# Splitting the squares of every query and key tile of the two dilated mixers into two fp32r parts, with the sum and the norm one share later

## The chip, the cores and the metric

One core of a Trainium2 chip runs the whole program. The metric is the device time of one execution in microseconds, the median of three runs. TensorE (PE) multiplies matrices, VectorE (DVE), ScalarE (ACT) and GpSimd (POOL) do the elementwise work, and SyncE (SP) issues the weight loads. Each engine works through its own instructions in order and waits on semaphores.

## The reference

The model is a trunk of four layers on 512 tokens of width 1024. The token mixers of layers 0 to 3 are dilated window attention (A), sparse attention (B), gated DeltaNet (C) and A again; each layer ends in a squared-ReLU MLP. The change concerns only the queries and keys of the A mixers, which are normalised per head:

```
def rms_norm(x, gain):
    y = x * lax.rsqrt(jnp.mean(x * x, axis=-1, keepdims=True) + EPS)
    return y * gain

def mixer_a(h, w_in, q_gain, k_gain, w_out, bias_tab):
    qkv = (h @ w_in).reshape(B, S, 3, A_N_GROUPS, A_HEADS, HEAD_DIM)
    q = rms_norm(qkv[:, :, 0], q_gain)
    k = rms_norm(qkv[:, :, 1], k_gain)
    v = qkv[:, :, 2]
    for g, (window, dilation) in enumerate(A_GROUPS):
        o, lse = dilated_window_attention(q[:, :, g], k[:, :, g], v[:, :, g], ...)
    wts = softmax(lses over the three groups)
    return sum(wts * outs) @ w_out
```

## The kernel before

**Weights.** A chunk of fp32 weights is loaded into `raw`. ACT copies it to `w_hi` in fp32r (L777, `rounding`), and POOL puts the rest, `raw - w_hi`, into `w_lo` in four pieces (L620, `split`). A product is then three fp32r matmuls for each block: `w_hi` with the high part of the activations, `w_hi` with the low part, and `w_lo` with the high part (L1916 in the A mixer).

**An A mixer.** There are four pairs of heads. Each pair has six tiles of 128 x 512: a query and a key tile for each of three groups, so 24 tiles in a mixer. The first six ("opening") and the values come first. The other 18 tiles are then projected between the steps of the attention. I number them tile 0 to tile 17, in order. A tile is 24 matmuls. The work is cut into 52 *shares* G of 8 or 9 matmuls, two in each *step* s of the attention loop: `fill(2s)` and `fill(2s+1)`. A tile ends in every third share, with two exceptions: the 18 tiles end in shares 2, 5, 8, 11, 14, 17, 20, 23, 25, 28, 31, 34, 37, 40, 43, 46, 49 and 51. `a_ended(i, G)` names the tile that ends in share G.

**A step on PE** is: `weigh(s-3)` (probabilities times values, L2205), `scores(s)` (L2162 near, L2169 far), `turn(s-2)` (transposes, L2189), `fill(2s)`, `fill(2s+1)`, then in some steps from 26 on a piece of the output projection (`joined`, L1962), and in steps 9, 17, 25 and 33 `difference` (L2219), which spreads the log-sum-exps of a pair's groups over `stat_bank`, PSUM bank 7. Step 28 has no filling work, and in steps 27 and 29 it is only `joined`.

**The norm of a tile**: ACT squares it from PSUM into the one buffer `asq`, that is `sq0` (L902, `qk_tile`), and copies the tile itself out (L903). DVE adds the epsilon term in place (L1378, `add_eps`). PE sums the squares over each head with a matrix of 128 x 128 (`sum_qk`). ACT takes the logarithm and then the exponential with -0.5 (L927 and L929, `qk_rms`), and POOL multiplies the tile by the result (L634, `qk_scale`). In the 18 tiles of the steps the sum is one fp32 matmul (L2092), issued at the end of the share after the one in which the tile ends. In the six opening tiles ACT makes an fp32r copy of the squares (L920, `sq_high`) in a spare slice of `g_hi`, DVE writes the rest (L1384, `sq_low`) to `g_lo`, and PE sums the two with two fp32r matmuls (L2088, L2089).

**`stat_bank` is shared.** A sum waits until the logarithm of the tile before has read the bank (`qln_done`), and after a `difference` until DVE has read it (`aclamp_done`, L1433, `clamped`). A `difference` waits for the logarithm of the last sum issued.

**The order around the steps on ACT**: copies of turned probabilities (L1017, from step 26), `probs(s)` (the exponentials of the attention, L977), in steps 10, 18, 26 and 34 three operations of 128 x 512 that make the mixing weights of a pair (L1026, L1028, L1030), `part(2s)`, `part(2s+1)`, and in steps 12, 20, 28 and 36 the high part of the pair's output (L1035). `part(G)` does the norm of the tile that ended a share before, then squares and copies the tile that ends in G, then rounds the next weights if a chunk is done. On DVE a step is: reciprocals (L1410), from step 25 on the scaling of probabilities (L1441), outputs (L1420), `logits(s)` (L1401), `part(2s)`, copies of turned probabilities up to step 25 (L1501), `part(2s+1)`, `clamped`, low part of the output (L1460).

## Time and profile before

| | |
|---|---|
| median of 3 runs | 2767.97 us (2767.09 to 2771.35) |
| the profiled execution | 2773.47 us, of which the span from first to last instruction is 2771.7 us |
| PE busy | 2716.1 us, 98% of the span |
| POOL / ACT / DVE busy | 1359.7 (49%) / 1086.8 (39%) / 1046.8 us (38%) |
| chain that ended last | PE 91%, DVE 3%, ACT 2%, POOL 2% |
| fp32 sums L2092 | 72 matmul records for the 36 sums of the two A mixers, 592 ns each |

Two matmul records make up one fp32 sum. A record's length contains the way through the array, so neighbouring records overlap; what a matmul costs PE is read from the distance of the starts or from the chain. Times of the trace count from the start of the span. In layer 0 the steps run from 130.7 us to about 330 us.

### The profile page before, as it was taken

What the parts mean: (1) busy time and instruction counts of PE and PEld (TensorE: products, weight loads), DVE (VectorE), ACT (ScalarE), POOL (GpSimd) and SP (SyncE); (2) the same over time, 40 slices, a digit from 0 to 9 for tenths busy, and PEclk for the clock granted to TensorE, in tenths of its full rate; (3) what the DMA queues carried; (4) which work ended last, traced back from release to release, by engine and by line L of the source; (5) the groups of instructions that cost most, each with busy time, mean ns of one, the idle gap of its engine ahead of it and who ended that gap; (6) DMA issues with size and microseconds to landing.
All of it is one profiled execution on the core that took longest, in us unless ns stands there. A gap on an engine that the chain in (4) does not pass through costs nothing.

```text
span 2771.7 us, 37296 instructions
## 1 busy us (share of the span) xinstructions
PE 2716.1 (98%) x14594; PEld 2193.4 (79%) x14594; DVE 1046.8 (38%) x1966; ACT 1086.8 (39%) x1649; POOL 1359.7 (49%) x1042
## 2 busy tenths in 40 slices
PE   8999999999999999999899999999999999999999
PEld 6977688888766788888788887888888977688887
DVE  4044622113486512213777874311123044622112
ACT  5355633223446423324334344322234355533222
POOL 4577354445455354445444442445455576345443
PEclk9999999999999999999899999999999999999999
DMA  4322122323422123223312110232323322122232
GB/s 143 99 69 63 52 92 91 106 91 92 106 46 77 61 92 106 91 91 110 80 33 57 37 62 24 92 98 91 106 91 99 100 54 69 56 97 91 92 105 76
DMA packets 273439, 227.87 MB, mean 82 GB/s; under 512 B 29220, under 2 KB 260388, under 8 KB 273300
## 3 DMA queue, kind: packets, MB, share of 16 engines
q1 hardware_dynamic: 262578, 216.66, 25.9%
q10 hardware_dynamic: 10722, 9.28, 1.5%
q8 instruction: 96, 1.57, 0.2%
q14 instruction: 43, 0.35, 0.0%
HBM read 223.62 MB, written 2.30 MB: 82 GB/s over the span
## 4 chain that ended last, share of the span: by engine, by line
PE 91%; DVE 3%; ACT 2%; POOL 2%; issue 1%; DMA 1%; ACTq 0%; SPq 0%; DVEq 0%; POOLq 0%
PE bank L2009 50%; PE bank L1916 20%; PE bank L2132 4%; PE bank L2372 2%; PE bank L2512 2%; PE bank L2092 1%; PE bank L2189 1%; PE bank L2205 1%; POOL w_lo L620 1%; PE bank L1962 1%; PE bank L2169 1%; PE bank L2162 1%; PE bank L2219 1%; POOL arena L693 1%; PE bank L1943 1%
## 5 line engine op out<-in xcount | busy, mean ns | idle before, releaser
L620 POOL TENSOR_TENSOR w_lo<-raw,w_hi 128x512 fp32r<-128x512 f32 x808 | 1081.0, 1368 | 1087.0 <-ACT w_hi L777 1067.7
L777 ACT ACTIVATE w_hi<-raw 128x2048 fp32r<-128x2048 f32 x201 | 383.7, 1909 | 462.1 <-PE bank L2009 423.3
L2009 PE MATMUL bank<-h_hi,w_hi 128*128 128x512 f32 x1024 | 400.8, 391 | 0.0
L2009 PE MATMUL bank<-g_hi,w_hi 128*128 128x512 f32 x1024 | 398.6, 389 | 0.0
L2009 PE MATMUL bank<-h_hi,w_lo 128*128 128x512 f32 x1024 | 398.4, 389 | 0.0
L2009 PE MATMUL bank<-g_hi,w_lo 128*128 128x512 f32 x1024 | 398.4, 389 | 0.0
L2009 PE MATMUL bank<-h_lo,w_hi 128*128 128x512 f32 x1024 | 398.4, 389 | 0.0
L2009 PE MATMUL bank<-g_lo,w_hi 128*128 128x512 f32 x1024 | 398.4, 389 | 0.0
L1916 PE MATMUL bank<-h_hi,w_hi 128*128 128x512 f32 x776 | 317.3, 409 | 2.4 <-POOL w_lo L620 1.9
L1916 PE MATMUL bank<-h_lo,w_hi 128*128 128x512 f32 x776 | 310.5, 400 | 0.0
L1916 PE MATMUL bank<-h_hi,w_lo 128*128 128x512 f32 x776 | 307.8, 397 | 0.0
L847 ACT ACTIVATE arena<-arena 128x512 f32<-128x512 f32 x128 | 80.9, 632 | 425.8 <-DVE arena L1345 425.8
L1345 DVE SCALAR_TENSOR_TENSOR arena<-bank,rs 128x512 f32<-128x512 f32 x128 | 88.5, 691 | 372.7 <-PE bank L2009 349.2
L1360 DVE TENSOR_TENSOR x<-x,bank 128x512 f32<-128x512 f32 x96 | 66.0, 687 | 431.6 <-PE bank L2009 431.6
L2009 PEld LDWEIGHTS bank<-h_hi,w_hi 128*128 128x128 f32 x1024 | 192.2, 188 | 41.0 <-issue 1.4
L2009 PEld LDWEIGHTS bank<-h_lo,w_hi 128*128 128x128 f32 x1024 | 192.2, 188 | 41.0 <-issue 1.4
L2009 PEld LDWEIGHTS bank<-h_hi,w_lo 128*128 128x128 f32 x1024 | 192.2, 188 | 40.2
L2009 PEld LDWEIGHTS bank<-g_hi,w_lo 128*128 128x128 f32 x1024 | 192.2, 188 | 40.2
L2009 PEld LDWEIGHTS bank<-g_lo,w_hi 128*128 128x128 f32 x1024 | 192.2, 188 | 39.8
L2009 PEld LDWEIGHTS bank<-g_hi,w_hi 128*128 128x128 f32 x1024 | 192.2, 188 | 39.7
L1916 PEld LDWEIGHTS bank<-h_hi,w_hi 128*128 128x128 f32 x776 | 147.5, 190 | 40.0 <-issue 10.4
L1916 PEld LDWEIGHTS bank<-h_lo,w_hi 128*128 128x128 f32 x776 | 147.6, 190 | 35.1 <-issue 6.9
(276 smaller groups left out, 3805.0 us busy)
## 6 DMA issues: line engine op xcount, KB each, us to landing
raw<-in_mlp_w SPq DMA_DIRECT2D x128, 1024.0 KB, 5.4
raw<-in_a_w_in SPq DMA_DIRECT2D x48, 512.0 KB, 5.1
raw<-in_c_w_in SPq DMA_DIRECT2D x32, 512.0 KB, 5.5
raw<-in_a_w_in SPq DMA_DIRECT2D x12, 1024.0 KB, 5.2
raw<-in_b_w_in SPq DMA_DIRECT2D x18, 256.0 KB, 4.0
raw<-in_a_w_out SPq DMA_DIRECT2D x4, 1024.0 KB, 4.9
raw<-in_b_w_in SPq DMA_DIRECT2D x4, 1024.0 KB, 5.4
arena<-bias_scratch ACTq DMA_DIRECT2D x16, 256.0 KB, 3.6
```

Source lines behind the costliest of these rows:

```text
L620: ins = nc.gpsimd.tensor_tensor(w_lo[s][:, k, :], raw[s][:, k, :], w_hi[s][:, k, :].bitcast(F32), ALU.subtract)
L693: nc.gpsimd.tensor_tensor(btm[t % 2][:, :, 0:n], bbias[f % 2][:, :, TOK - n:TOK], score[b].unsqueeze(1).to_broadcast([P, 2, n]), ALU.add). ...
L777: nc.scalar.activation(w_hi[s][:], raw[s][:], ACT.Copy).then_inc(w_hi_done, 1)
L847: nc.scalar.activation(gsq[j % 2], relu_t[j % 2], ACT.Square).then_inc(gsq_done, 1)
L1345: nc.vector.scalar_tensor_tensor(relu_t[j % 2], lin_bank[j % 2][:], 0.0, rs, ALU.max, ALU.mult).then_inc(relu_done, 1)
L1360: nc.vector.tensor_tensor(x[:, c, :], x[:, c, :], lin_bank[c % 2][:], ALU.add).then_inc(x_added, 1)
L1916: mm = nc.tensor.matmul(o, lhsT, rhs, start=start, stop=stop)
L1943: mm = nc.tensor.matmul(stat_bank[:], ones, sq[c % 2], start=c == 0, stop=c == CT - 1)
L2009: mm = nc.tensor.matmul(lin_bank[j][:], w[s][:, c, P * j:P * j + P], a[:, c, :], start=c + z == 0, stop=c == CT - 1 and z == 2)
L2132: mm = nc.tensor.matmul(bank[2 + b][:], keys, quads[w][:, c, :], start=half + c + z == 0, stop=half == 1 and c == 3 and z == 2)
L2372: mm = nc.tensor.matmul(out[z:z + HD], lhsT[:, z:z + HD], rhs, start=start, stop=stop)
L2512: mm = nc.tensor.matmul(bk4(3)[:, c, :], atl[k % 3][:, c, :], Tm[:, c, :], start=True, stop=True)
```

## The change

All 24 tiles of an A mixer, and not only the six opening ones, are now summed as two fp32r parts. In the steps the parts are made so: ACT's `sq_high` one share after the tile's end (head of `part`), DVE's `sq_low` behind the copy of turned probabilities of the step (for the tiles of shares 2s-1 and 2s). PE's sum, ACT's `qk_rms` and POOL's `qk_scale` move from one share behind to two. The squaring of the next tile waits for `sq_low` instead of the sum.

```diff
--- before.py
+++ after.py
@@ -240,13 +240,13 @@
             y_first[i] = at_y
             at_y += {0: A_PAIRS, 1: B_PAIRS, 2: C_HEADS}[KINDS[i]]
 
-        opening = {}
+        in_parts = {}
         q_first, copy_first, at_q, at_c = {}, {}, 0, 0
         for i in layers:
             q_first[i], copy_first[i] = at_q, at_c
             if KINDS[i] == 0:
-                for k in range(6):
-                    opening[at_q + k] = len(opening)
+                for k in range(6 * A_PAIRS):
+                    in_parts[at_q + k] = len(in_parts)
             at_q += {0: 6 * A_PAIRS, 1: 10, 2: 0}[KINDS[i]]
             at_c += {0: 12, 1: 8, 2: 2 + 4 * C_HEADS}[KINDS[i]]
 
@@ -449,7 +449,7 @@
 
         def sq_parts(Q):
 
-            return g_hi[:, 4 + opening[Q] % 2, :], g_lo[:, 4 + opening[Q] % 2, :]
+            return g_hi[:, 4 + in_parts[Q] % 2, :], g_lo[:, 4 + in_parts[Q] % 2, :]
 
         def a_stat(f, k):
 
@@ -648,7 +648,7 @@
                                                 ALU.mult).then_inc(an_done, 1)
 
                 def part(G):
-                    for k, n, t in a_ended(i, G - 1):
+                    for k, n, t in a_ended(i, G - 2):
                         qk_scale(0, a_q(i, k, n, t), a_qk_tile(k, t - tile0[n]))
 
                 def share(s, lo, hi):
@@ -894,9 +894,9 @@
                     src, blocks = reversed_blocks(src), by_block
                 act.wait_ge(lin_done, t + 1)
                 sqs = mem[kind]["sq"]
-                if Q in opening:
-                    if opening[Q]:
-                        act.wait_ge(qlo_done, opening[Q])
+                if Q in in_parts:
+                    if in_parts[Q]:
+                        act.wait_ge(qlo_done, in_parts[Q])
                 elif Q - q_base(kind) >= len(sqs) or (Q and len(sqs) == 1):
                     act.wait_ge(ssq_done, Q - len(sqs) + 1)
                 nc.scalar.activation(blocks(sqs[Q % len(sqs)]), src, ACT.Square).then_inc(qsq_raw, 1)
@@ -915,8 +915,8 @@
             def sq_high(Q):
 
                 act.wait_ge(qsq_done, Q + 1)
-                if opening[Q] >= 2:
-                    act.wait_ge(ssq_done, Q - 1 if opening[Q] % 6 >= 2 else Q)
+                if in_parts[Q] >= 2:
+                    act.wait_ge(ssq_done, Q - 1 if in_parts[Q] % (6 * A_PAIRS) >= 2 else Q)
                 nc.scalar.activation(sq_parts(Q)[0], mem[0]["sq"][0], ACT.Copy).then_inc(qhi_done, 1)
 
             def qk_rms(kind, Q):
@@ -963,9 +963,12 @@
 
                 def part(G):
                     for k, n, t in a_ended(i, G - 1):
+                        sq_high(a_q(i, k, n, t))
+                    for k, n, t in a_ended(i, G):
+                        qk(k, n, t)
+                    for k, n, t in a_ended(i, G - 2):
                         qk_rms(0, a_q(i, k, n, t))
                     for x in a_ended(i, G):
-                        qk(*x)
                         ended(*x)
 
                 def probs(u):
@@ -1380,7 +1383,7 @@
             def sq_low(Q):
 
                 hi, lo = sq_parts(Q)
-                dve.wait_ge(qhi_done, opening[Q] + 1)
+                dve.wait_ge(qhi_done, in_parts[Q] + 1)
                 nc.vector.tensor_tensor(lo, mem[0]["sq"][0], hi.bitcast(F32), ALU.subtract).then_inc(qlo_done, 1)
 
             def mixer_a(li, i):
@@ -1499,6 +1502,9 @@
                             dve.wait_ge(apv_done, U0 + u - 2)
                         n = 2 * P * a_blocks(u)
                         nc.vector.tensor_copy(apt[u % 3][:, 0:n], bank[4 + u % 2][:, 0:n]).then_inc(at_copied, 1)
+                    for G in (2 * s - 1, 2 * s):
+                        for k, n, t in a_ended(i, G):
+                            sq_low(a_q(i, k, n, t))
                     part(2 * s + 1)
                     if s == A_UNITS + 3:
                         projected(s - 1)
@@ -2077,13 +2083,13 @@
 
             def sum_qk(kind, Q):
 
-                pe.wait_ge(qlo_done, opening[Q] + 1) if Q in opening else pe.wait_ge(qsq_done, Q + 1)
+                pe.wait_ge(qlo_done, in_parts[Q] + 1) if Q in in_parts else pe.wait_ge(qsq_done, Q + 1)
                 if Q:
                     pe.wait_ge(qln_done, Q)
                 if spread[0]:
                     pe.wait_ge(aclamp_done, spread[0])
                 summed[0] = Q + 1
-                if Q in opening:
+                if Q in in_parts:
                     hi, lo = sq_parts(Q)
                     nc.tensor.matmul(stat_bank[:], halves_r[:], hi, start=True, stop=False)
                     nc.tensor.matmul(stat_bank[:], halves_r[:], lo, start=False, stop=True).then_inc(ssq_done, 1)
@@ -2141,7 +2147,7 @@
                         a, b = max(lo, 24 * j), min(hi, 24 * j + 24)
                         if a < b:
                             tile(n, t, a - 24 * j, b - 24 * j)
-                    for k, n, t in a_ended(i, G - 1):
+                    for k, n, t in a_ended(i, G - 2):
                         sum_qk(0, a_q(i, k, n, t))
 
                 def scores(u):
```

On PE, at the end of step 9 in layer 0 (shares 18 and 19, then the first `difference`), the kernel before has:

```order
L2092 MATMUL bank<-sq,com 128x512 [waits qln_done,qsq_done]
L1916 MATMUL bank<-h_lo,w_hi 128x512
L1916 MATMUL bank<-h_hi,w_lo 128x512
L1916 MATMUL bank<-h_hi,w_hi 128x512
L1916 MATMUL bank<-h_lo,w_hi 128x512
L1916 MATMUL bank<-h_hi,w_lo 128x512
L1916 MATMUL bank<-h_hi,w_hi 128x512
L1916 MATMUL bank<-h_lo,w_hi 128x512
L1916 MATMUL bank<-h_hi,w_lo 128x512
L1916 MATMUL bank<-h_hi,w_hi 128x512
L2219 MATMUL bank<-com,arena 64x128 [waits qln_done,alse_done]
L2219 MATMUL bank<-com,arena 64x128 x15
```

Nine projection matmuls (share 19) stand between the sum of tile 5 and the `difference`. The same place in the changed kernel:

```order
L1922 MATMUL bank<-h_lo,w_hi 128x512
L1922 MATMUL bank<-h_hi,w_lo 128x512
L1922 MATMUL bank<-h_hi,w_hi 128x512
L2094 MATMUL bank<-g_hi,halves_r 128x512 [waits qln_done,qlo_done]
L2095 MATMUL bank<-g_lo,halves_r 128x512
L2225 MATMUL bank<-com,arena 64x128 [waits qln_done,alse_done]
L2225 MATMUL bank<-com,arena 64x128 x15
```

The sum now stands directly ahead of the `difference`. The same has happened in step 25 with the sum of tile 16; at the second `difference`, in step 17, it is the other way round: there the sum of tile 11 stood directly ahead of it, and has moved behind it.

On ACT, steps 25 and 26 of layer 0, that is from the exponentials of step 25 to the norm of tile 17, the kernel before has:

```order
L977 ACTIVATE arena<-arena 128x256 [waits al_done] x2
L927 ACTIVATE sq<-bank 128x512 [waits qk_ready,ssq_done]
L929 ACTIVATE sq<-sq 128x512 [waits qln_done]
L902 ACTIVATE sq<-bank 128x512 [waits ssq_done,lin_done]
L903 ACTIVATE arena<-bank,par 128x512
L777 ACTIVATE w_hi<-raw 128x2048 [waits lin_done,raw_loaded1]
L1017 ACTIVATE arena<-bank 128x512 [waits apv_done,at_turned]
L977 ACTIVATE arena<-arena 128x256 [waits al_done] x2
L1026 ACTIVATE rs<-ss 128x512 [waits aclamp_done]
L1028 ACTIVATE rs<-rs,com 128x512 [waits aexp_done]
L1030 ACTIVATE rs<-rs 128x512 [waits aexp_done]
L927 ACTIVATE sq<-bank 128x512 [waits qk_ready,ssq_done]
```

The norm of tile 16 (first L927, L929) stands ahead of the square of tile 17 (L902). In the changed kernel (three lines later in the file, so L1030 is L1033; L920 is `sq_high`):

```order
L920 ACTIVATE g_hi<-sq 128x512 [waits ssq_done,qsq_done]
L902 ACTIVATE sq<-bank 128x512 [waits qlo_done,lin_done]
L903 ACTIVATE arena<-bank,par 128x512
L927 ACTIVATE sq<-bank 128x512 [waits qk_ready,ssq_done]
L929 ACTIVATE sq<-sq 128x512 [waits qln_done]
L777 ACTIVATE w_hi<-raw 128x2048 [waits lin_done,raw_loaded1]
L1020 ACTIVATE arena<-bank 128x512 [waits apv_done,at_turned]
L980 ACTIVATE arena<-arena 128x256 [waits al_done] x2
L1029 ACTIVATE rs<-ss 128x512 [waits aclamp_done]
L1031 ACTIVATE rs<-rs,com 128x512 [waits aexp_done]
L1033 ACTIVATE rs<-rs 128x512 [waits aexp_done]
L920 ACTIVATE g_hi<-sq 128x512 [waits ssq_done,qsq_done]
```

The norm of tile 16 has moved behind the square and the copy of tile 17, and the high part of tile 17's squares, which the sum now needs, stands behind the three mixing operations of step 26.

## Rows read from the trace of the kernel before

**Rows 1.** The page, first section: busy time, share of the span, instructions.
```profile
PE 2716.1 (98%) x14594; PEld 2193.4 (79%) x14594; DVE 1046.8 (38%) x1966; ACT 1086.8 (39%) x1649; POOL 1359.7 (49%) x1042
```
**Rows 2.** Windows: steps of both mixers; us, then PE, PEld, DVE, ACT, POOL.
```profile
130.00:290.00 160.00, 158.33 (x940) 115.87 (x938) 70.22 (x211) 88.52 (x192) 112.10 (x100) 1.00 0.26 66
...
2150.00:2360.00 210.00, 208.33 (x1154) 165.18 (x1153) 70.21 (x211) 102.33 (x206) 135.17 (x119) 1.00 0.27 73
```
**Rows 3.** Chain of waits, steps 11 to 18: start, length, what.
```profile
205.12 1.84 PE bank L1916 x8
206.95 0.86 PE bank L2092 x2
...
240.38 0.87 PE bank L2092 x2
...
241.28 0.61 ACT sq L927
241.88 0.14 issue
242.02 1.97 PE bank L2219 x32
```
**Rows 4.** Chain of waits, opening tile: the two-part sum.
```profile
42.37 0.23 PE bank L2088
42.60 0.24 PE bank L2089
```
**Rows 5.** Timeline of PE, the sum of tile 6, with idle time and releaser.
```profile
196.69 1.13 PE L2092 MATMUL bank<-sq,com 128*128 128x512 f32 x2 [0.89 <-DVE sq L1378]
```
**Rows 6.** Source lines L920, L1384, L1378: shortest/median/longest in ns.
```profile
L920 ACT ACTIVATE g_hi<-sq x12: 615/630/633, 36.3 to 2136.0; 128x512 fp32r<-128x512 f32 x12
...
L1384 DVE TENSOR_TENSOR g_lo<-sq,g_hi x12: 692/807/1373, 37.0 to 2136.6; 128x512 fp32r<-128x512 f32 x12
...
L1378 DVE TENSOR_TENSOR sq<-sq,em x48: 672/1128/2173, 35.6 to 2363.9; 128x512 f32<-128x512 f32 x48
```
**Rows 7.** Timeline of ACT, unit 13 (tile 8) and step 19 (tile 12).
```profile
214.45 0.49 ACT L977 ACTIVATE arena<-arena 128x256 f32<-128x256 f32 x1
...
248.63 0.58 ACT L902 ACTIVATE sq<-bank 128x512 f32<-128x512 f32 x1
...
251.57 0.49 ACT L977 ACTIVATE arena<-arena 128x256 f32<-128x256 f32 x1
```
**Rows 8.** Timeline of PE, starts of steps 14 and 20.
```profile
216.13 0.66 PE L2205 MATMUL bank<-arena 128*64 128x128 f32 x8
...
255.35 0.66 PE L2205 MATMUL bank<-arena 128*64 128x128 f32 x8
```
**Rows 9.** Timeline of ACT, end of step 25 and step 26.
```profile
292.48 0.60 ACT L902 ACTIVATE sq<-bank 128x512 f32<-128x512 f32 x1 [0.79 <-PE bank L1916]
...
293.54 1.91 ACT L777 ACTIVATE w_hi<-raw 128x2048 fp32r<-128x2048 f32 x1
...
298.80 0.63 ACT L1030 ACTIVATE rs<-rs 128x512 f32<-128x512 f32 x1
299.34 0.58 ACT L927 ACTIVATE sq<-bank 128x512 f32<-128x512 f32 x1
```
**Rows 10.** Timeline of PE, steps 25 to 29.
```profile
292.37 1.97 PE L2219 MATMUL bank<-com,arena 128*64 128x128 f32 x32
294.17 0.61 PE L2205 MATMUL bank<-arena 128*64 128x128 f32 x8
...
295.61 1.02 PE L2092 MATMUL bank<-sq,com 128*128 128x512 f32 x2
...
302.45 0.72 PE L2169 MATMUL bank<-arena 64*128 64x128 f32 x8 [0.67 <-POOL arena L634]
...
304.44 0.66 PE L2205 MATMUL bank<-arena 128*64 128x128 f32 x8 [0.69 <-ACT arena L1017]
...
306.96 0.47 PE L1962 MATMUL bank<-g_hi,w_hi 128*128 128x512 f32 x1 [0.64 <-DVE g_lo L1460]
```

## The prediction

> **What bounds the kernel now.** I began with the page. PE is busy 98% of the span [rows 1], and the other engines half of it or less, so an instruction taken off PE counts in full unless PE then waits for something. The windows over the steps of the two A mixers say the same: of 160 us in the first, PE is busy 158.3, ACT 88.5, DVE 70.2 and POOL 112.1 [rows 2]. So the copies that the change gives to ACT and DVE have room on average. Whether they have room where they stand is another question, since every engine works in order. The chain of waits shows it: from step 11 to 18 it runs through PE alone, with one exception, where PE waits for a logarithm on ACT ahead of a `difference` [rows 3]. After that I read the timelines around each tile's sum, and above all around step 26.
>
> **What goes: the fp32 sums.** Each takes 0.86 us of PE in the chain [rows 3], there are 36 (18 in each mixer). The two-part sum of the opening tiles takes 0.23 + 0.24 = 0.47 us [rows 4]. That is 0.39 us each, 36 x 0.39 = 14.0 us less on PE. The price on the others: 36 `sq_high` of 0.63 us = 22.7 us on ACT and 36 `sq_low` of 0.69 us (the shortest, without contention) = 25 us on DVE [rows 6], over the 370 us of [rows 2], in which ACT idles for 179 and DVE for 230. No DMA changes its place in a queue; SP's loads wait only for the weight split. The opening tiles and layers 1 and 2 keep their order.
>
> **Waits that go.** The sum of tile 6 waits 0.9 us for DVE's add, because the square stands behind the mixing operations of step 10 [rows 5]; a share later that is covered. The 0.8 us ahead of the second `difference` (from the end of the sum to 242.02, [rows 3]) go, since the sum of tile 11 moves behind it. Together 1.7 us in a mixer, 3.4 us.
>
> **Waits that come, the first difference.** The sum of tile 5 now stands directly ahead of the `difference` of step 9. That is the situation of [rows 3], and costs the same 0.8 us: 1.6 us for both mixers. The bounds are 0 (if the logarithm of the tile were early, which its place right behind the sum excludes) and 1.3 us, if the exponentials of a step stand ahead of it on ACT; I take the row's value.
>
> **Waits of the ordinary sums.** A sum used to need square and add; it now needs square, add, `sq_high` and `sq_low`, and has one share more time, 1.84 us for 8 matmuls, two with the next attention part. For tiles that end in an even share `sq_high` follows at once. For the others it stands behind the exponentials of the next step, and `sq_low` behind a copy. The tight ones are:
> Tile 8: the exponentials end at 214.94 [rows 7], so the parts are ready at 214.94 + 0.63 + 0.69 = 216.26. PE gets there where step 14 begins, 216.13 [rows 8], less 0.86 for the sum that no longer stands before, plus 0.47 for tile 7's sum, which now comes in between: 215.74. That is 0.5 us of waiting, and a little more, because the norm of tile 7 now stands ahead of the output's high part in step 12. I take 0.7.
> Tile 12: the norm of tile 11 (1.2 us of ACT) moves between the mixing operations and the square at 248.63 [rows 7]. The exponentials of step 19 then end at 252.06 + 1.2, the parts at 254.6 or, with the mix of the outputs ahead on DVE, up to 255.4; PE arrives at 255.35 - 0.86 = 254.5 [rows 8]. I take 0.5. Tile 10 comes out level, 0.1. The rest have 0.5 us or more to spare by the same count.
> Together 1.3 us, or 2.6 us. Bounds: 0 (they were all covered), and 3.5 us in a mixer, if `sq_low` takes its longest, 1.37 us [rows 6], in five of them. The value lies near the shortest duration, since only some meet POOL.
>
> **Step 25 and 26, the dear place.** Three things come together. (a) The sum of tile 16 now stands directly ahead of the third `difference`, exactly where tile 17 ends, call it T (292.37 [rows 10]). ACT first squares and copies tile 17 and is free at 293.54 [rows 9], T + 1.17; only then comes the logarithm of tile 16, until T + 1.92 with the gap of [rows 3]. PE is done with the sum at T + 0.47, so it waits 1.45 us; before, it did not wait. (b) Call the start of step 26 W (294.17 before). The mixing operations hang on the `difference`, and ACT is free of them at 299.34 [rows 9], W + 5.17. Only then come `sq_high` of tile 17 (0.63) and `sq_low` (0.69): ready at W + 6.54. PE arrives at the sum at 295.61, W + 1.44 [rows 10], since there is no projection left to do in shares 52 and 53. It stands for 5.1 us, and the first pieces of the output projection, which do not need tile 17, stand behind the sum on PE. (c) In return a later wait goes. Before, the far scores of step 28 waited 0.67 us for tile 17's scaling. From the sum's end PE has 302.45 - 0.67 - 296.47 = 5.3 us of its own work until there, and logarithm, exponential and scaling need about 2.6. The waits of 0.69 and 0.64 us behind it [rows 10] hang on turns, copies and exponentials of steps 28 and 29 and move along with PE. So the place costs 1.45 + 5.1 - 0.7 = 5.85 us, 11.7 for both mixers. Bounds for one mixer: from below 1.0 + 4.0 - 2.0 = 3.0 us, if ACT gets through a us sooner and the three later waits all melt; from above 1.45 + 5.8 = 7.25 us with the longest `sq_low` and nothing back.
>
> **Sum.** -14.0 - 3.4 + 1.6 + 2.6 + 11.7 = -1.5 us, against the profiled execution's 2773.47 us: 2772.0. That execution is 5.5 us above the median of the runs, 2767.97; the same difference there gives 2766.5 us.
>
> **A rule that speaks against the change.** The add on DVE takes 0.67 us at the shortest and 1.13 in the middle, up to 2.17, and `sq_low` 0.69 to 1.37 [rows 6]. The Trainium skill (SBUF — State Buffer, "SBUF: two separate sides") says why that could be: a VectorE operation with two SBUF inputs and a GpSimd operation take the shared ports as an exclusive lock for a whole instruction. By that rule, with which the spread in the rows agrees, each added `sq_low` also holds POOL up.
>
> **The rivals.**
> *The waits melt (faster).* The chain of before already leaves PE between 295.8 and 307 and goes through ACT and DVE, so a late sum may in part lie beside time that was lost anyway. If the waits of 0.67, 0.69 and 0.64 all go (2.0 us) and the ordinary sums are covered: -14.0 - 3.4 + 1.6 + 2 x (1.45 + 5.1 - 2.0) = -6.7, or 2761 us. For it: there is one more share of time, and the other engines idle half of the steps. Against: the copies and exponentials behind the last two waits are counted from PE's own turns.
> *DVE and POOL collide (slower).* Place: the tight tiles 1, 8, 10, 12, 16 and 17. `sq_low` takes 1.37 instead of 0.69 us, and sums that had no slack wait it out: 12 x 0.7 = 8.2 us over the forecast, 2774.7 us. It is slower than before as soon as more than two sums in three at these places are hit. Against it: at tile 17's place POOL waits itself, for the norm; in the rows half of the 12 `sq_low` took 0.81 us or less.
> *The sum doesn't get cheaper.* Two matmuls with both weights loaded anew could cost more beside a projection than in the opening. The rows show 0.47 us directly behind projection matmuls, so hardly; with no saving at all it would be 2780 us.
>
> **How the numbers follow.** The forecast has 0.55, the melting waits 0.27, the collision 0.16, the last 0.02. About 0.2% of the time, 5.5 us, is what a measurement of this kernel can tell from no change; so faster is below 2762.4 and slower above 2773.5. The forecast's own bounds go from 2756.6 (-14.0 - 3.4 + 0 + 0 + 6.0 = -11.4) to 2773.7 (-14.0 - 3.4 + 1.6 + 7.0 + 14.5 = +5.7), but its corners are unlikely. Of the forecast 0.1 lies on the faster side and little on the slower one; of the melting case four fifths are faster; of the collision four fifths slower. Faster 0.29, same 0.55, slower 0.16. For 8 in 10 I take 2758 to 2774 us.
>
> **What would show it.** Right, if in the profile after: the 36 two-part sums stand in the chain with 0.47 us each; PE waits about 5 us ahead of the high-part matmul of tile 17, once in each mixer, for DVE's `g_lo` or, behind it, ACT's `g_hi`; PE waits 1.4 us ahead of the third `difference` and 0.8 ahead of the first; the wait ahead of the far scores of step 28 is gone. Wrong, if the wait at tile 17 is under 3 us, or if ordinary sums wait more than 3.5 us in a mixer, or if POOL's split comes late and projection matmuls wait for `w_lo`.

## The result, and the profile after

The changed kernel takes 2793.18 us (median of 6 runs, 2790.88 to 2794.08), the kernel before 2768.88 us beside it (6 runs). The ratio is 1.0085, with an interval from 1.0072 to 1.0098. That is 24.3 us slower. The forecast was 2766.5 us, in a range from 2758 to 2774. The profiled executions lie 17.4 us apart (2790.88 and 2773.47 us): the one of before was above its median, the one of after below. What follows accounts for those 17.4 us. Part of the other 6.9 goes with the clock: the profiled execution of before had a mean granted clock of 0.993. Beside the experiments 4 of 57 executions of that kernel had 0.993 and took 2771.3 to 2775.1 us, while most had 0.995 and took 2766.9 to 2771.5. The rest is open.

The page of the kernel after, first section, which answers to [rows 1]:

```profile
PE 2708.3 (97%) x14594; PEld 2195.1 (79%) x14594; DVE 1085.3 (39%) x2002; ACT 1105.0 (40%) x1685; POOL 1367.3 (49%) x1042
```

PE is busy 7.8 us less, where 14.0 were forecast (part of the gap are matmuls at a lower clock, shown below), and the span is 17.4 us longer: about 25 us more of waiting. The window over the steps of the first A mixer, which answers to the first of [rows 2] (PE, PEld, DVE, ACT, POOL, then the granted clock):

```profile
130.00:290.00 160.00, 153.27 (x941) 116.17 (x941) 85.09 (x223) 95.56 (x204) 117.99 (x100) 1.00 0.24 65
```

PE was busy 158.3 of these 160 us and is now busy 153.3. DVE went from 70 to 85 us, ACT from 89 to 96, and POOL, which got no work, from 112 to 118. The waits of PE in the kernel after, summed by line and releaser (us in total, times, longest):

```profile
PE bank L2094 <- DVE g_lo L1387: 22.8, 8, 6.6
...
PE bank L2225 <- ACT sq L927: 3.8, 4, 1.1
PE bank L2211 <- DVE arena L1504: 3.3, 4, 1.3
```

In the kernel before, the sums of these tiles waited 1.8 us in all, two waits of 0.9 [rows 5]. They now wait 22.8 us for the low part. Where, in layer 0, the timeline of PE after shows (start, length, what, idle time and releaser; the waits up to step 24 but for one of 0.22 us at 158.29, then steps 25 and 26):

```profile
140.46 0.44 PE L2195 MATMUL bank<-com,arena 128*128 128x128 f32 x2 [0.25 <-POOL arena L647]
...
176.47 0.66 PE L2195 MATMUL bank<-com,arena 128*128 128x128 f32 x4 [0.50 <-POOL arena L647]
...
188.44 0.77 PE L2225 MATMUL bank<-com,arena 128*64 128x128 f32 x10 [0.78 <-ACT sq L927]
...
196.74 0.44 PE L2211 MATMUL bank<-arena 128*64 128x128 f32 x4 [1.25 <-DVE arena L1504]
...
215.94 0.50 PE L2094 MATMUL bank<-g_hi,halves_r 128*128 128x512 f32 x1 [1.43 <-DVE g_lo L1387]
...
222.77 0.66 PE L2211 MATMUL bank<-arena 128*64 128x128 f32 x8 [0.38 <-DVE arena L1504]
...
255.36 0.50 PE L2094 MATMUL bank<-g_hi,halves_r 128*128 128x512 f32 x1 [1.85 <-DVE g_lo L1387]
...
292.67 0.50 PE L2094 MATMUL bank<-g_hi,halves_r 128*128 128x512 f32 x1 [1.54 <-DVE g_lo L1387]
...
294.52 0.73 PE L2225 MATMUL bank<-com,arena 128*64 128x128 f32 x9 [1.11 <-ACT sq L927]
...
304.51 0.79 PE L2094 MATMUL bank<-g_hi,halves_r 128*128 128x512 f32 x1 [6.59 <-DVE g_lo L1387]
```

Three kinds of wait are to be seen. Sums wait for `g_lo` (215.94, 255.36, 292.67, 304.51). Turns and `weigh` wait for POOL and for DVE's copy, which they did not do before; 196.74 is the place of [rows 5], where the sum's own wait of 0.89 us went and the next operation fed by the same mixing operations waits 1.25. And both `difference`s wait for a logarithm.

The expensive place is steps 24 to 26. The chain of waits there, kernel after (start, length, what):

```profile
283.12 0.24 PE bank L2094
283.36 0.24 PE bank L2095
...
283.62 0.61 ACT sq L927
...
285.40 1.78 DVE sq L1381
...
288.35 1.33 DVE arena L1444
...
291.38 0.53 ACT g_hi L920
...
291.93 0.70 DVE g_lo L1387
...
298.25 1.35 DVE arena L1444
...
303.12 0.62 ACT g_hi L920
...
303.77 0.70 DVE g_lo L1387
...
304.51 0.79 PE bank L2094
305.31 0.43 PE bank L2095
305.73 2.56 PE bank L1968 x6
...
310.35 1.40 PE bank L1968 x6
```

It reads as two loops through ACT and DVE where the kernel before had PE. The sum of tile 15 ends at 283.60. Its logarithm and exponential stand on ACT, then the square of tile 16, DVE's add, DVE's scaling, exponentials, `sq_high`, `sq_low`, and only then the sum of tile 16. The second loop, from the `difference` to the sum of tile 17, is the one that was forecast, but it is longer. The reason is in DVE's scaling of two tiles of probabilities. The timelines of step 26, the kernel before and then the kernel after:

```profile
295.18 0.62 DVE L1441 TENSOR_SCALAR arena<-arena 128x256 f32<-128x256 f32 x2
295.53 3.10 POOL L620 TENSOR_TENSOR w_lo<-raw,w_hi 128x512 fp32r<-128x512 f32 x2 [2.48 <-ACT w_hi L777]
```

```profile
296.91 2.53 POOL L620 TENSOR_TENSOR w_lo<-raw,w_hi 128x512 fp32r<-128x512 f32 x2 [0.52 <-ACT w_hi L777]
297.32 2.28 DVE L1444 TENSOR_SCALAR arena<-arena 128x256 f32<-128x256 f32 x2
```

In the kernel before the scaling starts 0.35 us ahead of POOL's split and takes 0.62 us. In the kernel after PE waits 1.11 us ahead of the `difference`. The scaling stands behind DVE's reading of the `difference` and the split does not, so now the split starts first, by 0.41 us, and the scaling takes 2.28 us. The last rows of the chain show something more: the same six matmuls of L1968 take 2.56 us behind the wait and 1.40 us five microseconds later. The windows of the kernel after at that place (columns as above):

```profile
300.00:304.00 4.00, 0.00 (x0) 0.00 (x0) 1.33 (x6) 3.48 (x8) 0.00 (x0) 0.81 0.00 0
304.00:308.00 4.00, 3.49 (x8) 2.48 (x8) 1.15 (x4) 1.23 (x2) 0.89 (x1) 0.50 0.00 0
308.00:312.00 4.00, 4.00 (x25) 2.56 (x26) 2.33 (x7) 1.57 (x5) 2.84 (x3) 0.83 0.00 0
```

PE stood still from 297.9 to 304.5, and the granted clock went from 1.00 to 0.50, that is from 2.4 to 1.2 GHz. In the kernel before it was 1.00 in all windows from 284 to 308.

The source lines after, which answer to [rows 6] (shortest, median, longest in ns):

```profile
L920 ACT ACTIVATE g_hi<-sq x48: 612/620/634, 36.2 to 2381.5; 128x512 fp32r<-128x512 f32 x48
...
L1387 DVE TENSOR_TENSOR g_lo<-sq,g_hi x48: 674/739/1374, 36.8 to 2382.2; 128x512 fp32r<-128x512 f32 x48
...
L1381 DVE TENSOR_TENSOR sq<-sq,em x48: 672/1245/2067, 35.4 to 2371.7; 128x512 f32<-128x512 f32 x48
```

### The profile page after: what moved, and what is told of

Its sections match the earlier page's. It is cut to its first block, busy times and chain, and to the rows that moved or that the text cites. A ratio compares the mean times of both kernels' runs of the same rounds, so it can differ in the third digit from the quotient of the medians.

```text
span 2789.1 us, 37404 instructions
## 1 busy us (share of the span) xinstructions
PE 2708.3 (97%) x14594; PEld 2195.1 (79%) x14594; DVE 1085.3 (39%) x2002; ACT 1105.0 (40%) x1685; POOL 1367.3 (49%) x1042
## 4 chain that ended last, share of the span: by engine, by line
PE 87%; DVE 4%; ACT 3%; POOL 3%; issue 2%; DMA 1%; ACTq 0%; SPq 0%; DVEq 0%; POOLq 0%
PE bank L2015 50%; PE bank L1922 18%; PE bank L2138 4%; PE bank L2518 2%; PE bank L2378 2%; POOL w_lo L620 2%; PE bank L1968 1%; PE bank L2195 1%; PE bank L2211 1%; POOL arena L647 1%; PE bank L2225 1%; POOL arena L693 1%; PE bank L1949 1%; PE bank L2175 1%; PE bank L2333 0%
```

## The experiments

The theory after the result: the cheaper sum is real, and waits eat it up, above all those of the sums for the low part. The rivals: the later place alone costs the time; the low part's work costs it, through DVE and POOL getting in each other's way; or the place at tile 17 is nearly all of it. Each kernel stands beside runs of the kernel before on the same chip (medians 2768.1 to 2769.6 us).

**e1_lag_only.** The kernel before with the sums still in fp32, only their place, the norm's and the scaling's moved from one share behind to two. ACT keeps the order of the kernel before in `part`: where the two meet, a norm stands ahead of the next tile's square (tiles 7 and 8, 16 and 17), which the kernel after has the other way round, and a square still waits for the sum of the tile before.

```diff
-                    for k, n, t in a_ended(i, G - 1):
+                    for k, n, t in a_ended(i, G - 2):
                         sum_qk(0, a_q(i, k, n, t))
...
```

> Only the order of the change: the sums stay fp32 (0.86 us), no high and low parts are made, but sum, norm and scaling stand two shares behind instead of one. Theory L (the later place is the cost: the scaling blocks POOL's queue ahead of the scaling of probabilities, so turns wait, and the norms push the squares back on ACT): 8 to 12 us slower than before, turns waiting for POOL's L647 in steps 5 and 8 as in the changed kernel. Theory W (the added work on ACT and DVE is the cost, through their queues and the chain at tile 17): within 3 us of before, no wait of a turn for POOL. In both, tile 17's sum must not wait, since it needs no parts, so the gap of about 8 us at step 26 is gone.

Measured: 2782.40 us, ratio 1.0039 (1.0025 to 1.0053), 12.8 us slower than before. The later place, with that order on ACT, costs by itself about as much as the cheaper sums were to save. The size is near theory L, but its mechanism is not the one at work: turns wait for POOL only 0.5 us in all. Counted from step 0, PE's scores are 1.1 us later than before at step 24 and 6.7 at step 31, so most of it is lost behind step 24.

**e2_last_fp32.** The kernel after, with only tile 17 summed in fp32, without its parts.

```diff
-                for k in range(6 * A_PAIRS):
+                for k in range(6 * A_PAIRS - 1):
                     in_parts[at_q + k] = len(in_parts)
...
```

> The changed kernel, but with the last tile of each mixer (tile 17) summed in fp32 as before, without parts; 34 of 36 sums stay in two parts. Theory P (the place at tile 17 is the main loss: 8 us of waiting behind the mixing operations, and slower matmuls right behind it): 16 to 20 us faster than the changed kernel, so 4 to 8 us slower than before. Rival theory S (the loss is spread over many short waits and comes back elsewhere when one is removed): under 8 us faster than the changed kernel.

Measured: 2784.27 us, ratio 1.0051 (1.0031 to 1.0072), 8.9 us faster than after, or 4.5 us in a mixer. Theory P misses (16 to 20), and its rival too, by a little: tile 17's parts are about a third of the loss. PE still waits 1.54 us at tile 16, as in the kernel after, and then longer ahead of the third `difference`. Timeline of this kernel:

```profile
296.37 3.49 PE L2227 MATMUL bank<-com,arena 128*64 128x128 f32 x32 [1.90 <-ACT sq L927]
```

The wait is 1.90 us in place of 1.11, and the `difference` takes 3.49 us in place of 1.97 [rows 10]; the granted clock from 296 to 300 us was 0.57.

**e3_parts_no_lag.** The kernel after, with sum, norm and scaling one share behind, as in the kernel before.

```diff
-                    for k, n, t in a_ended(i, G - 2):
+                    for k, n, t in a_ended(i, G - 1):
                         sum_qk(0, a_q(i, k, n, t))
...
```

> The parts for all tiles, but sum, norm and scaling one share behind, as before the change. Theory L: the turns wait for POOL no more, but ordinary sums now come 1.9 to 2.3 us too early for their parts; tile 17 stays as in the changed kernel, since shares 52 and 53 hold no work. I expect 0 to 15 us slower than the changed kernel from 16 sums in a mixer waiting 0 to 1 us more, less about 3 us in a mixer from the turns. Theory W: clearly slower than the changed kernel, by more than 15 us, since the work on ACT and DVE bounds every sum.

Measured: 2842.29 us, ratio 1.0257 (1.0240 to 1.0274), 73 us slower than before and 49 slower than the kernel after. The waits of PE in this kernel, first row of the sums:

```profile
PE bank L2094 <- DVE g_lo L1387: 62.1, 36, 5.0
```

All 36 sums wait, 1.7 us on average. The parts need the second share. More than 15 us is what theory W forecast, and theory L fails here: the added work on ACT and DVE bounds every sum when it has one share. So both theories hold in part, L in e1 and W here.

**e4_one_part.** The kernel before, with nothing moved: DVE's add writes fp32r into the spare slice of `g_hi`, and PE sums it with one fp32r matmul. The low part of the squares is left out.

```diff
-                nc.vector.tensor_tensor(blocks(sq_), blocks(sq_), e, ALU.add).then_inc(qsq_done, 1)
+                out = g_hi[:, 4 + single[Q], :] if Q in single else sq_
+                nc.vector.tensor_tensor(blocks(out), blocks(sq_), e, ALU.add).then_inc(qsq_done, 1)
...
+                if Q in single:
+                    nc.tensor.matmul(stat_bank[:], halves_r[:], g_hi[:, 4 + single[Q], :], start=True,
+                                     stop=True).then_inc(ssq_done, 1)
+                    return
```

> The kernel before, with the 18 tiles of the steps summed by one fp32r matmul over squares that DVE's add writes as fp32r; the low part of the squares is left out. No work is added on any engine and nothing is moved. It asks what the fp32 sums are worth when nothing new is waited for: 36 x (0.86 - 0.23) = 22.7 us if PE is the bound everywhere in the steps. If steps 26 to 29 are bound by ACT and DVE as the chain before shows, the two or three last sums give nothing back: 19 to 22 us faster. If other engines bound the steps soon after PE gets faster (the changed kernel's profile speaks for that): only 8 to 15 us.

Measured: 2747.91 us, ratio 0.9914 (0.9898 to 0.9931), 21.7 us faster than before. From the durations of [rows 3] and [rows 4] it should be 36 x (0.86 - 0.23) = 22.7 us. So PE's time for a sum counts in full as long as nothing else moves: the price of the sum in the forecast was right. It is the fastest kernel of this study, with less of the computation.

**e5_high_only.** The kernel after without `sq_low` in the steps: ACT's high part alone is summed, with one matmul, two shares behind. The low part of the squares is left out.

```diff
-                    for G in (2 * s - 1, 2 * s):
-                        for k, n, t in a_ended(i, G):
-                            sq_low(a_q(i, k, n, t))
...
+                elif Q in in_parts:
+                    pe.wait_ge(qhi_done, in_parts[Q] + 1)
```

> The changed kernel without DVE's part: the 18 tiles of the steps are summed by one fp32r matmul over ACT's high copy; the low part of the squares is left out. Order and ACT's work are those of the changed kernel. It splits the loss of the ordinary sums. Theory D (DVE's in-order queue: it stands still for ACT's high part, and all behind it comes late): the waits of turns for POOL in steps 5 and 8 and of tiles 8 and 12 go; 36 x 0.23 = 8 us from the matmuls plus about 8 to 12 us of waits: 16 to 20 us faster than the changed kernel. Theory A (ACT's work and the later place are the cost, DVE's is not): only the matmuls and the 0.7 us of the low part at tile 17, 8 to 11 us faster.

Measured: 2771.66 us, ratio 1.0012 (1.0003 to 1.0022), 21.5 us faster than after, more than either theory had. The wait at tile 12 is gone and the one at tile 8 falls from 1.43 to 0.86 us. Timeline of this kernel, the places of tiles 16 and 17:

```profile
286.71 0.49 PE L2101 MATMUL bank<-g_hi,halves_r 128*128 128x512 f32 x1 [0.81 <-ACT g_hi L924]
288.56 3.52 PE L2234 MATMUL bank<-com,arena 128*64 128x128 f32 x32 [1.35 <-ACT sq L931]
...
298.05 0.80 PE L2101 MATMUL bank<-g_hi,halves_r 128*128 128x512 f32 x1 [4.54 <-ACT g_hi L924]
```

Even the high part alone comes too late there; the low part adds 0.7 us to the first wait. The last wait is 2.1 us shorter than in the kernel after, but mostly because the `difference` takes 3.52 us here and 1.97 there, so that PE comes later. From the start of the `difference` to the sum of tile 17 it is 9.5 us here and 10.0 in the kernel after, so the low part adds 0.5. In all its sums wait 12.3 us, in the kernel after 22.8.

**e8_one_part_late.** e4 with sum, norm and scaling two shares behind, and ACT's order as in e1. The low part of the squares is left out.

```diff
 (on top of e4)
-                    for k, n, t in a_ended(i, G - 1):
+                    for k, n, t in a_ended(i, G - 2):
                         sum_qk(0, a_q(i, k, n, t))
...
```

> The kernel that sums one fp32r part made by DVE's add (low part left out; it was 21.7 us faster than before), with sum, norm and scaling two shares behind instead of one. No work is added anywhere, so the difference to that kernel is the price of the later place alone. With fp32 sums that price was 12.8 us. Theory: it hangs on the third difference and steps 25 to 29, not on the length of the sum, so again 10 to 14 us slower than the one-part kernel, 8 to 12 us faster than before. Rival: cheap sums leave slack, price under 5 us.

Measured: 2763.88 us, ratio 0.9983 (0.9973 to 0.9993), 16 us above e4. No sum waits for its squares here; `weigh`s do. Timeline of this kernel, steps 26 and 27, PE, DVE and POOL:

```profile
290.07 2.57 POOL L622 TENSOR_TENSOR w_lo<-raw,w_hi 128x512 fp32r<-128x512 f32 x2 [1.58 <-ACT w_hi L779]
290.19 2.59 DVE L1444 TENSOR_SCALAR arena<-arena 128x256 f32<-128x256 f32 x2
293.23 0.44 PE L2212 MATMUL bank<-arena 128*64 128x128 f32 x4 [1.14 <-DVE arena L1423]
298.10 0.66 PE L2212 MATMUL bank<-arena 128*64 128x128 f32 x8 [1.70 <-ACT arena L1019]
```

The same scaling and split in e4:

```profile
285.77 0.62 DVE L1444 TENSOR_SCALAR arena<-arena 128x256 f32<-128x256 f32 x2
...
286.12 3.11 POOL L622 TENSOR_TENSOR w_lo<-raw,w_hi 128x512 fp32r<-128x512 f32 x2 [2.50 <-ACT w_hi L779]
```

In e4 the scaling starts 0.35 us ahead of the split and takes 0.62 us. In e8 it starts 0.12 us behind the split and takes 2.59 us, to within 0.2 us of the split's end. It comes later because DVE first has to add the epsilon term to tile 17's squares (287.65 to 289.50). The square (287.04) stands behind tile 16's norm on ACT, and the add takes 1.85 us in place of 1.13. The `difference` itself also waits 0.78 us for a logarithm. Outputs, logits, exponentials and the next `weigh`s come that much later; e4's two `weigh`s waited 0.74 and 0.69 us. So the later place costs without any part, and at step 26 through DVE and POOL getting in each other's way. The kernel after turns ACT's order round at this place and so does not have this one link, but the order of split and scaling flips there too. Counted from step 0, e8 falls behind e4 by 1.9 us up to step 24 and by 6.4 up to step 31. e1 shows the same waits, 0.54, 1.67 and 1.63 us at three `weigh`s.

**e9_low_no_wait and e10_wait_no_low.** Both are e5 with one half of what `sq_low` does to DVE. The low part of the squares is left out of the sum. e9 has the subtraction of 128 x 512, on other data, waiting for nothing of the tile; e10 waits for `sq_high` at the place of `sq_low` and then does an operation of 8 columns.

```diff
 (e9)
...
+                            nc.vector.tensor_tensor(g_lo[:, 6, :], em, em, ALU.subtract).then_inc(dead, 1)
 (e10)
+                            dve.wait_ge(qhi_done, in_parts[a_q(i, k, n, t)] + 1)
+                            nc.vector.tensor_tensor(g_lo[:, 6, 0:8], em[:, 0:8], em[:, 0:8], ALU.subtract)
```

> The kernel that sums only ACT's high part (3.5 us slower than before, 21.5 faster than the changed one), with a subtraction of DVE's added where `sq_low` stood: same shape, two inputs in SBUF, but it waits for nothing and nobody waits for it. It shows what the mere work of `sq_low` on DVE costs, its contention with POOL included. Theory C (contention and occupied DVE time are what costs): 5 to 10 us slower than the high-only kernel. Theory Q (DVE standing still for ACT's high part costs): under 3 us slower.

> The high-only kernel with DVE's wait for ACT's high part at the place of `sq_low`, followed by an operation on 8 columns in place of 512; nobody waits for it. It shows what the wait in DVE's queue costs without the work. Theory Q: 5 to 10 us slower than the high-only kernel, as reciprocals, outputs and logits behind it come late. Theory C: under 3 us slower. If both additions cost little, the price of the low part is the chain itself (sum after low part after high part) and the second matmul.

Measured: 2774.93 us, ratio 1.0022 (1.0013 to 1.0031), and 2774.03 us, ratio 1.0019 (1.0010 to 1.0028). That is 3 and 2 us over e5, and the intervals overlap with e5's. Theory C misses in e9 (5 to 10) and theory Q in e10. Neither DVE's work nor its waiting, each added alone, makes up much of the 21.5 us that lie between e5 and the kernel after. In e9 more turns wait for POOL than in e5. PE's waits in e9, the row of the turns:

```profile
PE bank L2210 <- POOL arena L649: 2.2, 4, 0.8
```

In e5 that line has 0.5 us in 2 waits, in the kernel after 1.9 in 6. In e10, which has the wait without the work, it is 0.5 in 2 again. So the waits for POOL in the kernel after come from DVE's added work, but they are small.

**e6_two_fp32_early.** The kernel after, with tiles 16 and 17 in fp32 and one share behind, as before.

```diff
+        def a_due(i, G):
+
+            tiles = a_tiles(i)
+            late = [x for x in a_ended(i, G - 2) if x not in tiles[-2:]]
+            return late + [x for x in a_ended(i, G - 1) if x in tiles[-2:]]
...
-                    for k, n, t in a_ended(i, G - 2):
+                    for k, n, t in a_due(i, G):
                         sum_qk(0, a_q(i, k, n, t))
```

> The changed kernel with tiles 16 and 17 of each mixer as before the change: fp32 sum, sum, norm and scaling one share behind. Tiles 0 to 15 keep parts and the later place. Summing tile 17 alone in fp32 gave only 9 us, since the sum of tile 16 still stood ahead of the third difference. Theory P (all that is lost from step 24 on comes from where these two tiles' sums stand): by the starts of step 24 the changed kernel is 0.7 us ahead of before in a mixer, and from there this kernel should run as before, so 0 to 3 us faster than before, 22 to 26 us faster than the changed kernel. Rival: the loss moves on and lands at tile 15 or at the scores of step 28: 5 to 10 us slower than before.

Measured: 2777.44 us, ratio 1.0033 (1.0022 to 1.0045). A miss: it is 9.3 us slower than before, though the dear place is as it was. Its steps start 1.1 us later than in the kernel before at step 24, and 6.2 us later at step 31 (start of PE's scores, counted from step 0). At step 24 the kernel after was 0.7 us ahead with the same instructions up to there: the sum of tile 12 waits 2.34 us here, not 1.85, and the granted clock from 256 to 260 us is 0.66. Behind step 24 stand waits like those of e1:

```profile
300.10 0.44 PE L2223 MATMUL bank<-arena 128*64 128x128 f32 x4 [0.53 <-DVE arena L1434]
304.97 0.66 PE L2223 MATMUL bank<-arena 128*64 128x128 f32 x8 [1.67 <-ACT arena L1031]
...
308.87 1.12 PE L2223 MATMUL bank<-arena 128*64 128x128 f32 x8 [1.19 <-DVE arena L1434]
```

Tile 15, still late, was suspected: its norm pushes on the work of steps 24 and 25. e11 tries that.

**e11_six_fp32_early.** The same with tiles 12 to 17 in fp32 and one share behind.

```diff
 (on top of e6)
-            late = [x for x in a_ended(i, G - 2) if x not in tiles[-2:]]
+            late = [x for x in a_ended(i, G - 2) if x not in tiles[-6:]]
...
```

> The changed kernel with its last six tiles (12 to 17) of a mixer in fp32 and one share behind, as before the change; tiles 0 to 11 keep parts and the later place. With only tiles 16 and 17 put back, 9 us remained, and its chain starts at the later sum of tile 15, whose norm pushes the square of tile 16 and brings DVE's scaling together with POOL's. Theory P: with tile 15 early too, steps 24 to 29 run as before. At the start of step 18 the changed kernel is 1.4 us ahead in a mixer; so 0 to 4 us faster than before. Rival (the loss moves ahead to whatever tile is the last late one): 3 us or more slower than before.

Measured: 2767.93 us, ratio 0.9996 (0.9987 to 1.0006). The timeline of this kernel, steps 28 and 29, has the waits of the kernel before [rows 10] again, 0.67 and 0.69 there:

```profile
302.24 0.72 PE L2187 MATMUL bank<-arena 64*128 64x128 f32 x8 [0.68 <-POOL arena L640]
304.23 0.66 PE L2223 MATMUL bank<-arena 128*64 128x128 f32 x8 [0.69 <-ACT arena L1031]
```

It is 0.8 us below its kernel before, where e6 is 9.3 above its own: tiles 12 to 15, with their parts and their later place, cost those 10 us. Whether it is the parts or the place, and whether tile 15 alone does it, was not tried. With 24 of the 36 sums in two parts, which saves PE 24 x 0.39 = 9.4 us, the kernel is as fast as before: waits take all but 0.8 of it.

**e7_high_first.** The kernel after, with `sq_high` of tile 17 ahead of the three mixing operations of step 26.

```diff
                     if z == 2 and f:
+                        for k, n, t in a_ended(i, 2 * s - 1):
+                            sq_high(a_q(i, k, n, t))
                         act.wait_ge(aclamp_done, F0 + f)
...
```

> The changed kernel, with one operation moved: in step 26 ACT makes the high part of tile 17 ahead of the three mixing operations (some 2 us) and not behind them. Theory P1 (PE's wait of 6.6 us at tile 17 hangs on those three operations): the wait falls to between 4 and 5 us; the mixing operations come 0.6 us later, which the path to the output of the pair pays back in part; with the clock falling less, 2 to 5 us faster than the changed kernel. Rival (the wait hangs on the exponentials of step 26 and on the norm of tile 16, the mixing operations being hidden): within 1 us of the changed kernel.

Measured: 2788.42 us, ratio 1.0067 (1.0050 to 1.0084), 4.8 us faster than after, within the forecast; the intervals overlap. Two of the four executions, at a mean granted clock of 0.993, took 2785.4 and 2785.7 us; the other two, at 0.990, took 2791.1 and 2791.3. All six of the kernel after had 0.990 or 0.991 and took 2790.9 to 2794.1. So some 2 us come at the same clock, and the rest where the clock fell less. The timeline of this kernel in layer 0:

```profile
306.06 0.79 PE L2097 MATMUL bank<-g_hi,halves_r 128*128 128x512 f32 x1 [4.66 <-DVE g_lo L1390]
```

4.66 us in place of 6.59: the 1.9 us of the three mixing operations went, as forecast. What stays is the way through DVE, which scales until 303.08 beside POOL's split, and the exponentials until 304.76.

**The ladder.** In medians, each against the kernel before beside it: PE's fp32 sum becomes one fp32r matmul, -21.7 us (e4); sum, norm and scaling go one share later, to -4.2 (e8); ACT makes the high part, and its order in `part` is turned, to +3.5 (e5); the low part, to +24.3 (after). The steps between are 17.4, 7.8 and 20.8 us; with intervals of 3 to 5 us to either side of the ratios they are good to a few us. Of the last, 36 x 0.23 = 8.3 us are the second matmul. The sums wait 22.8 - 12.3 = 10.5 us longer in the profiles, but about 3 of that replace the time that the two slow third `difference`s of e5 took (3.5 us each in place of 2.0). The rest is not assigned.

## Why the prediction was wrong

The account for the mixer of layer 0, in us. The fourth `difference` starts at 322.74 in the kernel before and at 332.35 in the kernel after: 9.6 us. 2.2 us come back up to the second A mixer (its first scores start at 2201.51 and 2208.95), which adds 10.0: together the 17.4.

| step of the prediction | forecast | measured |
|---|---|---|
| 18 sums at 0.39 | -7.0 | -7.0 |
| waits that go (tile 6, second `difference`) | -1.7 | -1.7 |
| first `difference` | +0.8 | +0.8 |
| waits of ordinary sums, to step 24, with all else lost there | +1.3 | +6.9 |
| sum of tile 16 | 0 | +1.5 |
| third `difference` | +1.45 | +1.1 |
| sum of tile 17 | +5.1 | +6.6 |
| later waits that go | -0.7 | -0.9 |
| PE at half clock | 0 | +2.4 |
| sum | -0.75 | +9.7 (9.6 by the starts) |

**The price of the sum: right.** The chain has 0.24 + 0.24 us for it, and e4 confirms that PE's time counts in full.

**Waits that go: right in themselves, wrong in the balance.** The wait of [rows 5] went, but it had hidden that `weigh` hangs on the same mixing operations through DVE's copy, and that wait of 1.25 us is longer.

**"Waits of the ordinary sums": the step that failed most.** The forecast was 1.3 us in a mixer and 6.9 were measured: steps 0 to 24 fall 7.7 us short of the saving, less 0.8 for the first `difference`. The list of waits above gives 5.9 of them; 1.0 has no row. Two things failed. First, the sums themselves wait 3.3 us, 1.43 at tile 8 and 1.85 at tile 12 against 0.7 and 0.5. The mechanism was named, the size was not. It is not the duration of `sq_low`, which took 0.77 and 0.67 us at these two, near the shortest as the forecast had it. The forecast let PE arrive at 215.74 and 254.5 us; it arrived at 215.94 - 1.43 = 214.51 and 255.36 - 1.85 = 253.51, mostly because it was already ahead (0.7 us at step 13 and 0.9 at step 19, counted from step 0), and the count had left that out. At tile 12 the parts were ready only at 255.30, at the late end of the forecast. Second, turns and `weigh`s wait 2.6 us for POOL and for DVE's copy, which was not looked for at all. The two for DVE's copy (1.25 and 0.38) are in e1 and e8 too and come with the later place; those for POOL come with DVE's added work (e9). The sums' own 3.3 us are just under the 3.5 that the prediction named as its sign of being wrong, so the sign did not show.

**The dear place: mechanism right, size about half.** 5.85 us were forecast, 10.7 measured. e2 and e7 show that the wait of tile 17 hangs where the forecast said. Three things were missed. The sum of tile 16 was taken to be covered, but the norm of tile 15 stands ahead of its square and DVE's scaling ahead of its exponentials: the add took 1.78 us and the two scalings 2.39, beside POOL's split, against 1.13 and 0.51 at this place in the kernel before. At tile 17 the parts were forecast for 6.5 us behind the start of step 26 and came after 8.2 (303.77 + 0.69 - 296.29); that is the scaling of 2.28 us in place of 0.62. And PE came out of the wait at half its clock, 2.4 us: 0.75 for the sum, 1.16 for the six matmuls behind it, the rest for the `weigh`, scores and turns until 310.

**The later place as a cost of its own: not in the prediction.** It was counted only where a sum comes to stand ahead of a `difference`. e1 and e8 measure 13 and 16 to 17 us for it without any part, with ACT's old order; what it costs in the order of the kernel after was not run. The rival of melting waits fails in the kernel after itself: of the three waits that were to go, 0.67 went, 0.69 stayed and 0.64 became 0.42. The place could not be kept either (e3).

**The rivals.** The collision of DVE and POOL was forecast at 2774.7 us with a chance of 0.16. As the rival had it, it did not come: the four `sq_low`s in a mixer that a sum waited for took 0.77, 0.67, 0.69 and 0.69 us (tiles 8, 12, 16, 17), and the long ones of 1.34 to 1.36 fell on tiles 9, 11, 13 and 15, where there was time. e9 adds that all of its work costs near 3 us. But the collision decides at a place that the rival did not name, where DVE's scaling, unchanged, slides under POOL's split (step 26 of the kernel after, and e8). That the sum doesn't get cheaper is refuted by e4.

**Slips in the sums.** 5.17 + 0.63 + 0.69 is 6.49 and not 6.54. The chance of faster adds up to 0.27 and not 0.29. In the rival of the collision three hits of twelve already make the kernel slower than before, and it takes ten to pass 2773.5 us. None of them moves the forecast by more than 0.1 us.

**What stays open.** How much of the 6.9 us between the medians' difference and the profiles' is clock; the later place without ACT's old order; and which of the late norms among tiles 12 to 15 pushes the steps behind 24.

## What to carry to other kernels

Where PE is busy 98% of the span, the cover of every helper operation is a fraction of a microsecond. An operation that goes off PE for two on engines that are half idle is to be counted by the lateness of its result and of all that stands behind it in their queues, at each place. The count has to carry along how far ahead the waiting engine already is, and to ask which operations change their order against a neighbour that slows them. Moving a consumer one share later gives the new producers time, and takes it from whoever uses the consumer's result; measure the move alone first. When a wait goes, ask who else hangs on the same chain, since that one is next.

## What the runs showed of the hardware

**The clock falls inside a kernel.** Behind 6.6 us without a matmul the granted clock was 0.50 for 4 us, and 0.83 in the next window. It needs no single long wait: in e2 PE idled 1.54 and 1.90 us between 292.2 and 296.4 us, and the clock from 296 to 300 was 0.57. The same waits do not always give it. In e5 and e9 PE waits 0.8 and 1.35 us at the same place; the window behind, of e5 and then of e9:

```profile
288.00:292.00 4.00, 3.44 (x34) 3.47 (x36) 0.46 (x1) 2.84 (x3) 2.32 (x2) 0.57 0.33 114
```

```profile
288.00:292.00 4.00, 3.40 (x46) 2.69 (x46) 1.87 (x4) 2.84 (x4) 2.46 (x2) 1.00 0.28 97
```

The first, e5, falls to 0.57 and its `difference` takes 3.52 us; the second, e9, stays at 1.00 and needs 1.97. Single executions of one kernel differ in the same way: those of e7 took 2785.4 and 2785.7 us at a mean granted clock of 0.993, and 2791.1 and 2791.3 at 0.990.

**DVE beside POOL.** DVE's add of two SBUF tiles took from 672 to 2067 ns in one and the same execution, and one scaling of probabilities (L1444, 128 x 256) from 345 to 1350 ns, while ACT's copy of 128 x 512 stayed between 612 and 634 ns. At four places where the two engines meet it goes by who starts first. The two scalings took 0.62 us where they started 0.35 us ahead of POOL's split (the kernel before and e4), and 2.28 and 2.59 us where they started 0.41 and 0.12 us behind it (the kernel after and e8). The split of two took 3.10 and 3.11 us in the first case, 2.53 and 2.57 in the second. This agrees with the rule that the prediction drew on for the add alone: the Trainium skill (SBUF — State Buffer, "SBUF: two separate sides") counts a VectorE operation in a two-port mode, and not only one with two SBUF inputs, among those that take the shared ports against GpSimd for a whole instruction. The scaling has one tensor input. In which mode it ran no trace shows.
